# Five RMS norms of a two-layer encoder trunk: statistics and spread by transpositions, sums on VectorE, and another output norm

## The reference, cut to what matters

```python
def rms_norm(x, g):
    xf = x.astype(jnp.float32)
    y = xf * lax.rsqrt(jnp.mean(xf * xf, axis=-1, keepdims=True) + EPS)
    return (y * g.astype(jnp.float32)).astype(x.dtype)
    ...
    return rms_norm(x, norm_final)
```

## Time and profile before

| what | us |
|---|---|
| median of three runs | 1120.38 |
| the profiled execution's own time | 1119.78 |
| its span | 1117.7 |
| TensorE matmul busy | 1099.7 (98% of the span) |
| TensorE weight load busy | 916.3 |
| VectorE busy | 647.8 |
| GpSimd busy | 531.2 |
| ScalarE busy | 436.0 |
| mean granted TensorE clock | 0.996 of full |

### The profile page before, as it was taken

How to read it: one execution, slowest core, us unless ns; L and a number is a source line. 1 busy time by engine, 2 the same in 40 slices (tenths; PEclk the granted TensorE clock), 3 DMA queues, 4 the chain that set the end, 5 groups by cost and what they waited for, 6 DMA issues and landing times.

```text
span 1117.7 us, 15509 instructions
## 1 busy us (share of the span) xinstructions
PE 1099.7 (98%) x5199; PEld 916.3 (82%) x5199; DVE 647.8 (58%) x1064; ACT 436.0 (39%) x672; POOL 531.2 (48%) x415
## 2 busy tenths in 40 slices
PE   8999999999999999999999999999999999999996
PEld 6888888888888888887888888888888888888885
DVE  6576557666666632223877677666766666641113
ACT  6783433332222333233655555443323222232321
POOL 5567745444444455554333323353544444445552
PEclk9999999999999999999999999999999999999998
DMA  8273323322222233233222222132222222232302
GB/s 302 93 222 125 103 90 101 105 95 94 94 94 94 98 109 108 98 113 113 95 90 81 86 88 78 57 106 94 96 102 102 94 94 94 94 104 103 113 19 75
DMA packets 37875, 115.07 MB, mean 103 GB/s; under 512 B 4912, under 2 KB 7600, under 8 KB 37840
## 3 DMA queue, kind: packets, MB, share of 16 engines
q1 hardware_dynamic: 35520, 110.39, 29.2%
q10 hardware_dynamic: 2320, 4.21, 1.2%
HBM read 112.19 MB, written 6.59 MB: 106 GB/s over the span
## 4 chain that ended last, share of the span: by engine, by line
PE 38%; issue 32%; POOL 22%; ACT 3%; DVE 2%; DMA 1%; SPq 0%; POOLq 0%; DVEq 0%; ACTq 0%
PE bank L1224 13%; PE bank L1226 12%; PE bank L1225 12%; POOL wl L372 12%; POOL wl L371 10%; DMA x<-x_in 1%; ACT wh L465 1%; DVE x L1217 0%; ACT L498 0%; SPq L310 0%; DVE bank L913 0%; DVE axc L914 0%; DVE bank L912 0%; DVE bank L970 0%; POOLq L369 0%
## 5 line engine op out<-in xcount | busy, mean ns | idle before, releaser
L371 POOL TENSOR_TENSOR wl<-raw,wh 128x512 fp32r<-128x512 f32 x190 | 249.5, 1313 | 552.4 <-ACT wh L465 552.4
L1224 PE MATMUL bank<-xh,wh 128*128 128x512 f32 x976 | 383.0, 392 | 2.3 <-DVE xl L840 2.1
L1226 PE MATMUL bank<-xh,wl 128*128 128x512 f32 x976 | 380.1, 389 | 0.0
L1225 PE MATMUL bank<-xl,wh 128*128 128x512 f32 x976 | 380.0, 389 | 0.0
L465 ACT ACTIVATE wh<-raw 128x1024 fp32r<-128x1024 f32 x190 | 201.1, 1060 | 359.7 <-PE bank L1226 317.1
L372 POOL TENSOR_TENSOR wl<-raw,wh 128x512 fp32r<-128x512 f32 x190 | 259.6, 1366 | 0.0
L1224 PEld LDWEIGHTS bank<-xh,wh 128*128 128x128 f32 x976 | 183.3, 188 | 42.3 <-DVE xl L840 2.0
L1226 PEld LDWEIGHTS bank<-xh,wl 128*128 128x128 f32 x976 | 183.2, 188 | 38.4
L1225 PEld LDWEIGHTS bank<-xl,wh 128*128 128x128 f32 x976 | 183.4, 188 | 36.9
L1224 PE MATMUL bank<-ah,wh 128*128 128x512 f32 (+1 forms) x357 | 134.6, 377 | 0.0
L1226 PE MATMUL bank<-ah,wl 128*128 128x512 f32 (+1 forms) x357 | 134.4, 377 | 0.0
(11 more groups left out here) (202 smaller groups left out, 1157.9 us busy)
## 6 DMA issues: line engine op xcount, KB each, us to landing
raw<-weights SPq DMA_DIRECT2D x190, 512.0 KB, 3.2
bias_scratch<-ext_scratch SPq DMA_DIRECT2D x1, 4096.0 KB, 19.1
bias<-bias_scratch ACTq DMA_DIRECT2D x8, 512.0 KB, 3.7
x<-x_in SPq DMA_DIRECT2D x8, 256.0 KB, 6.1
out<-x SPq DMA_DIRECT2D x4, 384.0 KB, 2.8
raw<-weights SPq DMA_DIRECT2D x4, 256.0 KB, 5.9
out<-x SPq DMA_DIRECT2D x2, 256.0 KB, 2.1
lng<-ln_g SPq DMA_DIRECT2D x1, 256.0 KB, 8.4
```

The costliest lines, as they stand in the source:

```text
L371: nc.gpsimd.tensor_tensor(low[:, 0:FIRST], raw[:, c % RAW, 0:FIRST], high[:, 0:FIRST], ALU.subtract)
L1224: nc.tensor.matmul(dst, w_hi_part, m_hi, start=first, stop=False)
L1225: nc.tensor.matmul(dst, w_hi_part, m_lo, start=False, stop=False)
L1226: return nc.tensor.matmul(dst, w_lo_part, m_hi, start=False, stop=last)
```

## The change

It edits three things.

1. In norms 0 to 3 the statistics become four transpositions of `acc` into bank 7, after which VectorE sums the 128 values of each position (`tensor_reduce` of 128x512 to `var`, 128x4). ScalarE's root takes `var` with a scale of 1/1024. VectorE writes the mean into `mean_sq`, and `inverse_root` is four instructions. It takes its reciprocal in place.
2. The spread becomes four transpositions of the broadcast column.
3. In the output norm the two matmuls over `acc` are done apart and earlier (`final_sums`; those of the second half right behind the first half's spread), VectorE multiplies straight from the bank, a second pair of transpositions into bank 0 or 1 serves ScalarE's copy for GpSimd, GpSimd has two tiles and VectorE six, SP stores VectorE's tiles in two stores of three and ScalarE's queue those of GpSimd.

```diff
-OUT_POOL = 3
+OUT_POOL = 2
...
+POOL_SCALE_BANKS = [0, 1]
...
@@ sync
-                sp.wait_ge(out_dve, (KT - OUT_POOL) * half + 2)
-                sp.dma_start(out[:, OUT_POOL:OUT_POOL + 2, cols], x[:, OUT_POOL:OUT_POOL + 2, cols]).then_inc(out_done, 16)
-                sp.wait_ge(out_dve, (KT - OUT_POOL) * (half + 1))
-                sp.dma_start(out[:, OUT_POOL + 2:, cols], x[:, OUT_POOL + 2:, cols]).then_inc(out_done, 16)
-                sp.wait_ge(out_pool, OUT_POOL * (half + 1))
-                sp.dma_start(out[:, 0:OUT_POOL, cols], x[:, 0:OUT_POOL, cols]).then_inc(out_done, 16)
+                for n in range(2):
+                    tiles_out = slice(OUT_POOL + 3 * n, OUT_POOL + 3 * n + 3)
+                    sp.wait_ge(out_dve, 6 * half + 3 * n + 3)
+                    sp.dma_start(out[:, tiles_out, cols], x[:, tiles_out, cols]).then_inc(out_done, 16)
@@ scalar
             def statistics(norm):
-                act.wait_ge(stat_mm, norm + 1)
-                nc.scalar.activation(root, bank[STAT_BANK][:, 0:4], ACT.Sqrt, bias=eps).then_inc(root_done, 1)
+                act.wait_ge(var_done, norm + 1)
+                nc.scalar.activation(root, var, ACT.Sqrt, bias=eps, scale=1.0 / D).then_inc(root_done, 1)
...
-                act.wait_ge(spread_mm, 5 + half)
-                nc.scalar.activation(rstd[:, cols], stat[:, 0:HALF], ACT.Copy).then_inc(rstd_done, 1)
+                act.wait_ge(spread_pool, half + 1)
+                nc.scalar.activation(rstd[:, cols], bank[POOL_SCALE_BANKS[half]][:, 0:HALF], ACT.Copy).then_inc(rstd_done, 1)
+                act.wait_ge(out_pool, OUT_POOL * (half + 1))
+                act.dma_start(out[:, 0:OUT_POOL, cols], x[:, 0:OUT_POOL, cols]).then_inc(out_done, 16)
@@ vector
-                r, t = rstd_col[:, at], newt[:, at]
-                link(nc.vector.reciprocal(r, root[:, at]))
-                link(tt(t, r, r, ALU.mult))
-                link(stt(t, stat, EPS, t, ALU.add, ALU.mult))
-                link(ts(t, t, -0.5, 1.5, ALU.mult, ALU.add))
-                tt(r, r, t, ALU.mult).then_inc(col_done, 1)
+                r, t, start = rstd_col[:, at], newt[:, at], root[:, at]
+                link(nc.vector.reciprocal(start, start))
+                link(stt(t, stat, EPS, start, ALU.add, ALU.mult))
+                link(stt(t, t, -0.5, start, ALU.mult, ALU.mult))
+                stt(r, t, 1.5, start, ALU.add, ALU.mult).then_inc(col_done, 1)
 
             def statistics(norm):
+                dve.wait_ge(stat_mm, norm + 1)
+                nc.vector.tensor_reduce(var, bank[STAT_BANK][:].rearrange("p (j c) -> p j c", j=4), mybir.AxisListType.X,
+                                        ALU.add).then_inc(var_done, 1)
+                dve.wait_ge(var_done, norm + 1)
+                link(ts(mean_sq, var, 1.0 / D, None, ALU.mult))
                 dve.wait_ge(root_done, norm + 1)
-                inverse_root(bank[STAT_BANK][:, 0:4], slice(0, 4))
+                inverse_root(mean_sq, slice(0, 4))
...
-                dve.wait_ge(rstd_done, 5 + half)
+                dve.wait_ge(spread_mm, 5 + half)
+                scale = bank[FINAL_STAT_BANKS[half]][:, 0:HALF]
                 for m in range(OUT_POOL, KT - 1):
-                    tt(x[:, m, cols], x[:, m, cols], rstd[:, cols], ALU.mult).then_inc(out_dve, 1)
-                stt(last, last, gain(4, KT - 1), rstd[:, cols], ALU.mult, ALU.mult).then_inc(out_dve, 1)
+                    tt(x[:, m, cols], x[:, m, cols], scale, ALU.mult).then_inc(out_dve, 1)
+                stt(last, last, gain(4, KT - 1), scale, ALU.mult, ALU.mult).then_inc(out_dve, 1)
@@ tensor, statistics and spread_rstd
-                    ins = nc.tensor.matmul(bank[STAT_BANK][:, j:j + 1], acc[:, P * j:P * j + P], mean_w,
-                                           start=True, stop=True)
+                    ins = nc.tensor.transpose(bank[STAT_BANK][:, P * j:P * j + P], acc[:, P * j:P * j + P], ident[:])
...
-                    ins = nc.tensor.matmul(bank[STAT_BANK][:, P * j:P * j + P],
-                                           rstd_col[:, j:j + 1].to_broadcast([P, P]), ident[:], start=True, stop=True)
+                    ins = nc.tensor.transpose(bank[STAT_BANK][:, P * j:P * j + P],
+                                              rstd_col[:, j:j + 1].to_broadcast([P, P]), ident[:])
@@ tensor, end of ffn(1)
                             if half and kt == 5:
-                                final_statistics(0)
+                                final_sums(0)
+                                final_last(0)
                             if half and kt == 12:
                                 final_spread(0)
+                                final_sums(1)
...
-                    final_statistics(1)
+                    final_last(1)
                     final_spread(1)
 
+            def final_sums(half):
+                pe.wait_ge(x_acc, 5 * KT - 1)
+                for j in range(2):
+                    at = HALF * half + P * j
+                    nc.tensor.matmul(bank[FINAL_STAT_BANKS[half]][:, j:j + 1], acc[:, at:at + P], mean_w,
+                                     start=j == 0, stop=False)
+
+            def final_last(half):
                 pe.wait_ge(final_sq, half + 1)
                 for j in range(2):
                     at = HALF * half + P * j
-                    nc.tensor.matmul(stat[:, j:j + 1], acc[:, at:at + P], mean_w, start=True, stop=False)
-                    ins = nc.tensor.matmul(stat[:, j:j + 1], sq[:, 1, at:at + P], mean_w, start=False, stop=True)
+                    ins = nc.tensor.matmul(bank[FINAL_STAT_BANKS[half]][:, j:j + 1], sq[:, 1, at:at + P], mean_w,
+                                           start=False, stop=j == 1)
                 ins.then_inc(stat_mm, 1)
 
             def final_spread(half):
                 pe.wait_ge(col_done, 5 + half)
...
                 ins.then_inc(spread_mm, 1)
+                for j in range(2):
+                    r = rstd_col[:, 2 * half + j:2 * half + j + 1]
+                    ins = nc.tensor.transpose(bank[POOL_SCALE_BANKS[half]][:, P * j:P * j + P],
+                                              r.to_broadcast([P, P]), ident[:])
+                ins.then_inc(spread_pool, 1)
```

More of the change, by code:

```diff
@@ L139, in trunk @@
         sq = persistent("sq", [P, 2, T], F32)
-        small = persistent("small", [P, 72], F32)
+        small = persistent("small", [P, 80], F32)
         eps = small[:, 0:1]
@@ L157, in trunk @@
         idle_mix = small[:, 66:72]
+        var = small[:, 72:76]
+        mean_sq = small[:, 76:80]
         bn6 = persistent("bn6", [P, 4, 6], F32)
@@ L231, in trunk @@
         x_ready, x_hi, x_lo, x_sq, x_acc = (sem(n) for n in ("x_ready", "x_hi", "x_lo", "x_sq", "x_acc"))
-        stat_mm, root_done, col_done, spread_mm, rstd_done = (
-            sem(n) for n in ("stat_mm", "root_done", "col_done", "spread_mm", "rstd_done"))
+        stat_mm, var_done, root_done, col_done, spread_mm, rstd_done = (
+            sem(n) for n in ("stat_mm", "var_done", "root_done", "col_done", "spread_mm", "rstd_done"))
         dve_step, pool_step = sem("dve_step"), sem("pool_step")
@@ L253, in trunk @@
             sem(n) for n in ("ptr_mm", "ptr_hi", "ptr_lo", "av_mm", "o_half", "o_sum", "o_hi", "o_lo", "rsum_inv"))
-        final_mm, x_last, final_sq, out_dve, out_pool = (
-            sem(n) for n in ("final_mm", "x_last", "final_sq", "out_dve", "out_pool"))
+        final_mm, x_last, final_sq, spread_pool, out_dve, out_pool = (
+            sem(n) for n in ("final_mm", "x_last", "final_sq", "spread_pool", "out_dve", "out_pool"))
         def gain(norm, m):
@@ L1465, in ffn @@
                         ins.then_inc(final_mm, 1)
-                    final_statistics(1)
+                    final_last(1)
                     final_spread(1)
-            def final_statistics(half):
-                stat = bank[FINAL_STAT_BANKS[half]]
+            def final_sums(half):
                 pe.wait_ge(x_acc, 5 * KT - 1)
+                for j in range(2):
[3 more added lines that the diff above has]
+            def final_last(half):
                 pe.wait_ge(final_sq, half + 1)
@@ L1483, in final_spread @@
                     r = rstd_col[:, 2 * half + j:2 * half + j + 1]
-                    ins = nc.tensor.matmul(bank[FINAL_STAT_BANKS[half]][:, P * j:P * j + P],
-                                           r.to_broadcast([P, P]), ident[:], start=True, stop=True)
+                    ins = nc.tensor.transpose(bank[FINAL_STAT_BANKS[half]][:, P * j:P * j + P],
+                                              r.to_broadcast([P, P]), ident[:])
                 ins.then_inc(spread_mm, 1)
+                for j in range(2):
+                    r = rstd_col[:, 2 * half + j:2 * half + j + 1]
+                    ins = nc.tensor.transpose(bank[POOL_SCALE_BANKS[half]][:, P * j:P * j + P],
+                                              r.to_broadcast([P, P]), ident[:])
+                ins.then_inc(spread_pool, 1)
```

## The result

The changed kernel takes **1112.97 us** (median of six runs, 1112.58 to 1114.31) beside 1120.51 us for the kernel before in the same comparison (six runs, 1119.34 to 1122.86). The ratio is 0.9934, 95% interval 0.9924 to 0.9945: 7.5 us or 0.66% faster. The forecast was 1113.9 in a range of 1112.6 to 1116.2. The profiled execution took 1113.03 us with a span of 1111.2, 6.5 us less than the span before, which is the sum as it was worked out (its terms are compared further down; their errors cancel).

A forecast was written before the change was run, and what follows sets the result against it. TensorE, busy 1099.7 of 1117.7 us, was taken as the bound. Savings of 2.34 + 0.6 + 3.56 = 6.5 us turn 1119.78 into 1113.3; with 0.6 for the median, 1113.9 us, range 1112.6 to 1116.2.

The forecast's parts named there:

- Norms 1 to 3: Statistics and spread as transpositions save 0.78 us per norm without a new TensorE wait: 2.34 us in all.
- norm 0: First norm: the factor comes 0.6 us earlier (bounds 0 and 0.78), despite a new wait of 0.35 to 0.5.
- the end: Output norm behind the last large matmul: shorter chain and fewer bytes left, 3.56 us earlier (bounds 1.8 and 4.0).
- A group of transpositions: Statistics or spread on TensorE: four transpositions at 0.105 us each take 0.42 instead of 0.81 us.
- The chain: Between statistics and spread: 2.49 us with a reduction of 0.69, leaving 0.57 slack; at 1.38, TensorE waits 0.12 per norm.
- The scaling in norm 0: VectorE's 1/1024 scaling lies beside ScalarE's root and adds nothing; three later steps are exposed to GpSimd.
- The clock at the end: The output norm's spread runs 2.8 us behind the last large matmul, before the clock's fall at 3.9; otherwise 0.37 later.
- The median: The median of runs was put 0.6 us above the 1113.3 worked out for the profiled execution.

The follow-up runs named there:

- last version: Changed kernel with the second half's two early sums moved behind the last large matmul and eight more pad clearings at VectorE's start: 1111.95 us, ratio 0.9926.
- the sums in the wait: Changed kernel with the second half's two sums over acc moved from kt 12 to right behind the last large matmul: 1112.39 us, ratio 0.9935.
- the clearings: Changed kernel with eight more clearings of the pads at the very start of VectorE's program: one execution, 1113.61 us.
- output norm alone: Changed kernel with statistics and spread of norms 0 to 3 put back to matmuls: 1116.34 us, ratio 0.9969 to the kernel before.
- stores 1, 2, 3: Changed kernel with SP's stores of VectorE's six tiles cut as one, two and three tiles instead of three and three: 1112.55 us.

## Why the prediction was right, point by point

The mechanism held: fewer records in the norms without a wait behind them, and a shorter chain at the end. That the sum hit the measured 6.5 us is partly luck. Norms 1 to 3 gave 2.70 instead of 2.34, norm 0 gave 0.47 instead of 0.6 and the end 3.36 instead of 3.56; the errors of +0.36, -0.13 and -0.20 cancel.

- **A group of transpositions.** 0.42 was forecast, 0.36 measured, for `acc` and for the broadcast column. The rate was right (0.108 over 52), but the first large matmul behind a group starts closer than a rate times a count says: 52 take 5.60 and 4 take 0.36, which is 5.24 for 48, 0.109 each, and 0.08 less at the group's end. A norm gives 0.90 instead of 0.78.
- **The chain.** The reduction took 0.69, the value taken. ScalarE's root took 0.30 instead of 0.26 and the slack was 0.44 instead of 0.57. No wait in norms 1 to 3, and what a wait would cost was tried with two reductions.
- **Norm 0.** Forecast 0.6, measured 0.47, for another reason than given, so that the nearness is luck. The step said that GpSimd's instruction "hangs on nothing that changes" and must meet the first two-operand step. In the changed kernel's trace L373 ran from 24.02 to 25.33, and L861 at 25.87 took 0.17: nothing was held up, the factor came 0.94 earlier, and half of that was lost at the gap of 0.52, which the sum doesn't have. In the last version's trace L373 ran from 25.13 and L861 took 0.87. The mechanism is real, but where GpSimd's instruction lies beside VectorE's chain differs from one execution to the next, so a single trace can't say whether it strikes.
- **The scaling in norm 0, a term put at nothing.** The prediction counts three steps that GpSimd can hold up and lets the scaling by 1/1024 lie beside the root. In 6 of the 11 traces with the new statistics a small step of norm 0 was held up, until 0.02 to 0.03 us behind the end of GpSimd's instruction. In two it was L861 (0.83 and 0.87 us), in four the scaling, which reads one operand from SBUF (0.80 to 1.23 instead of 0.17), and the reciprocal behind it had to wait. TensorE then waited before the spread, 0.13 to 0.51 us (0.80 with two reductions, which lengthen the chain themselves). GpSimd, VectorE and TensorE in the timed run with the sums in the wait:

```profile
24.66 1.31 POOL L373 TENSOR_TENSOR wl<-raw,wh 128x512 fp32r<-128x512 f32 x1
24.76 1.23 DVE L870 TENSOR_SCALAR small<-small 128x4 f32<-128x4 f32 x1
...
26.85 0.41 PEld L1278 LDWEIGHTS bank<-ident,small 128*128 128x128 f32 x4 [0.51 <-DVE small L863]
```

- **The end.** Forecast 3.56, measured 3.36. From the last large matmul: root at 1.88 (forecast 1106.98 - 1104.58 - 0.46 = 1.94), spread at 2.98 (3.04), multiplies at 3.55 (3.46), GpSimd at 4.13 (4.13), end at 9.27 (9.10). Mis-sized were VectorE's start behind two transpositions (0.57 instead of 0.42) and the step of a multiply (0.33 instead of 0.32). The matmuls added at kt 12 cost 0.49 (0.46).
- **The clock at the end.** The claim that the spread runs ahead of its fall held in the changed kernel (clock 1.00 until 1106.00) but was luckier than it read. The 3.9 us of one trace, counted from the matmul's end (4.2 from its start), were taken as a constant. From the start of the last large matmul, between 2.3 and 4.8 us were seen in the eleven traces with the new end, and the spread comes at 2.98; in two of them the clock fell first.
- **The median.** I added 0.6 for other executions. The changed kernel's profiled execution lies 0.06 above its median, so that addition was not a property of the kernel; without it the forecast is 1113.3.

## What to carry to other kernels

A float32 matmul whose only work is to move or sum 128 columns cost two records here; a transposition, with the sum on a VectorE that has time, cost one, and the move is free while the chain stays shorter than the matmuls that cover it. An operation that stands ahead of large matmuls belongs into a wait of the same engine, if one follows close behind (0.49 us in the traces here; the times alone didn't separate it). Read a moving coincidence (another engine's transfer, the fall of the clock) from several traces before a term of a sum rests on it.

## What the runs showed of the hardware that was not expected

- VectorE stood idle for 0.52 us between two instructions that waited for nothing late. Eight small instructions ahead moved its place in the stream, and the gap vanished. An instruction packet on q14 moved as well, but it started 0.7 us behind the gap's end; the cause is open.
- A VectorE instruction of 128x4 with a single SBUF operand (TENSOR_SCALAR, L870) took 0.80 to 1.23 us instead of 0.17 beside GpSimd's TENSOR_TENSOR in four traces, as those with two SBUF operands did in others.
- The granted clock fell from 1.00 to 0.50 at different times behind the start of the last large matmul. In eight kernels whose TensorE program is the same from there on: 2.8 us (with the clearings), 3.3 (52 transpositions), 3.5 (output norm alone), 3.6 (factor from SBUF), 3.7 (stores 1, 2, 3), 4.1 (changed kernel), 4.7 (two reductions) and 4.8 (all stores on SP). With the sums in the wait: 2.3, 3.4 and 3.5. A fall before the spread costs 0.35 to 0.38 us: 9.62 to 9.65 from that matmul to the end instead of 9.27.
- A bracket of 0.38 us before a weight load cost TensorE 0.14, since a load that waits gives up its lead of 0.22 over its matmul.
